# Row norms passed on by tile, first loads in order of use, multiplications by zeros there, gating's share added by itself, maxima and exponentials of the attentions in another order

## Time and profile before

| | us |
|---|---|
| median of 3 runs | 1327.89 (1327.08 to 1332.82) |
| the profiled execution, own time | 1327.28 |
| its span, first to last instruction | 1325.5 |
| TensorE busy | 1283.7 |
| VectorE busy | 933.4 |
| ScalarE busy | 692.4 |
| GpSimd busy | 30.8 |

### The profile page before, as it was taken

One profiled execution on the slowest core, in us unless ns is written; L12 is line 12 of the kernel. 1 busy time (PEld: TensorE's weight loads), 2 busy tenths in 40 slices (PEclk: granted clock), 3 DMA queues, 4 the chain that ended last, 5 costly groups with the idle time before them and its releaser, 6 DMA issues.

```text
span 1325.5 us, 21900 instructions
## 1 busy us (share of the span) xinstructions
PE 1283.7 (97%) x8592; PEld 1170.9 (88%) x8592; DVE 933.4 (70%) x1667; ACT 692.4 (52%) x1137; POOL 30.8 (2%) x26
## 2 busy tenths in 40 slices
PE   7999998999989988999999999999999999999997
PEld 6889988998878778999999999999988888888886
DVE  5766556665456756899999777777767766677766
ACT  5565556664445655444454455555554455544554
POOL 0000040000010000000000000000000000000000
PEclk9999998999999999999999999999999999999999
DMA  7533465556655435567767656565667776666663
GB/s 246 171 114 128 128 191 157 179 189 187 194 161 185 143 99 175 154 198 229 231 215 231 222 191 202 184 205 191 199 238 272 245 244 246 244 244 243 236 242 110
DMA packets 72662, 260.55 MB, mean 197 GB/s; under 512 B 8224, under 2 KB 8864, under 8 KB 72304
## 3 DMA queue, kind: packets, MB, share of 16 engines
q1 hardware_dynamic: 71232, 255.25, 58.9%
q0 software_dynamic: 1040, 3.38, 0.8%
q10 hardware_dynamic: 288, 0.52, 0.1%
HBM read 240.25 MB, written 18.87 MB: 195 GB/s over the span
## 4 chain that ended last, share of the span: by engine, by line
PE 89%; ACT 4%; DVE 4%; issue 1%; DMA 1%; SPq 0%; ACTq 0%; DVEq 0%
PE ps L937 26%; PE ps L457 15%; PE ps L465 14%; PE ps L466 14%; PE ps L467 14%; PE ps L920 2%; PE ps L500 1%; ACT whi L974 1%; DVE wlo L1407 1%; DMA X<-in_x_dram 1%; PE ps L481 1%; PE ps L475 1%; PE ps L873 1%; DMA raw<-in_w_in_dram 1%; PE ps L493 0%
## 5 line engine op out<-in xcount | busy, mean ns | idle before, releaser
L1407 DVE TENSOR_TENSOR wlo<-raw,whi 128x1024 fp32r<-128x1024 f32 (+2 forms) x411 | 499.2, 1216 | 327.0 <-ACT whi L974 324.7
L974 ACT ACTIVATE whi<-raw 128x1024 fp32r<-128x1024 f32 (+2 forms) x421 | 441.9, 1051 | 441.3 <-PE ps L937 168.6
L465 PE MATMUL ps<-TH,whi 128*128 128x256 f32 x1536 | 441.6, 287 | 2.5 <-DVE TL L1416 1.3
L466 PE MATMUL ps<-TL,whi 128*128 128x256 f32 x1536 | 434.7, 283 | 0.0
L467 PE MATMUL ps<-TH,wlo 128*128 128x256 f32 x1536 | 434.6, 283 | 0.0
L465 PEld LDWEIGHTS ps<-TH,whi 128*128 128x128 f32 x1536 | 294.8, 192 | 3.1 <-issue 3.1
L466 PEld LDWEIGHTS ps<-TL,whi 128*128 128x128 f32 x1536 | 295.0, 192 | 0.0
L467 PEld LDWEIGHTS ps<-TH,wlo 128*128 128x128 f32 x1536 | 294.7, 192 | 0.0
L937 PE MATMUL ps<-whi,TH 128*128 128x512 f32 x512 | 199.3, 389 | 1.3 <-issue 1.3
L937 PE MATMUL ps<-whi,TL 128*128 128x512 f32 x512 | 199.2, 389 | 0.0
L937 PE MATMUL ps<-wlo,TH 128*128 128x512 f32 x512 | 199.2, 389 | 0.0
(11 more groups left out here) (292 smaller groups left out, 1304.3 us busy)
## 6 DMA issues: line engine op xcount, KB each, us to landing
raw<-in_expert_u_dram SPq DMA_DIRECT2D x128, 512.0 KB, 3.7
raw<-in_expert_v_dram SPq DMA_DIRECT2D x128, 512.0 KB, 3.8
raw<-in_w_up_dram SPq DMA_DIRECT2D x32, 512.0 KB, 3.6
raw<-in_w_down_dram SPq DMA_DIRECT2D x32, 512.0 KB, 4.2
acts<-stage SPq DMA_DIRECT2D x32, 512.0 KB, 3.9
stage<-acts SPq DMA_DIRECT2D x30, 512.0 KB, 3.3
raw<-in_w_in_dram SPq DMA_DIRECT2D x20, 512.0 KB, 4.2
raw<-in_w_gate_dram SPq DMA_DIRECT2D x16, 512.0 KB, 3.4
```

Source lines behind the costliest of these rows:

```text
L465: e.matmul(dst, whi[:, h, sl], xh[:, k, :], start=k == 0, stop=False)
L466: e.matmul(dst, whi[:, h, sl], xl[:, k, :], start=False, stop=False)
L974: e.activation(whi[:, u % NH, 0:n], raw[:, u % NR, 0:n], ACT.Copy).then_inc(*hi(u))
L1407: e.tensor_tensor(wlo[:, u % NH, 0:n], raw[:, u % NR, 0:n], whi[:, u % NH, 0:n].bitcast(F32), ALU.subtract).then_inc(*lo(u))
```

## The change

1. **Start.** The constants are loaded in two parts, the identity (64 KB) first and the rest behind the fourth weight unit; x's parts and units 0 to 3 are issued in order of use. ppc is issued by ACT; positions, mask and gain vector by POOL, but only once chunk x5 is cut. ACT loads its table at once (`warm`). TensorE multiplies zeros: eight matmuls of 512 columns before the first transposes and three behind them, into a bank that is not read. x is transposed two chunks at a time, and a unit of IN_A is multiplied high part first (waiting for `hi` alone), the wlo part last.
2. **Norms "out" and "down".** The last three units do tile 0 first (`staggered_end`), then tile 1. X is transposed, cut and waited for by tile, in 128 x 128 pieces, sixteen where there were eight of 128 x 256; tile 0's transposes stand between tile 1's last matmuls. The next product begins with tile 0 alone: for UP and QUERY by `pair`, which streams 128 columns of each of two units at once against a tile of rows, and then turns the result round (`turn_paired`); for IN2 by `high_rows` and `low_rows`. The squares of the plain norm behind them move some steps later.
3. **Norm "x4"** likewise by tile, with single roots and reciprocals; QUERY + 1's low part goes to POOL.
4. **Gating's share by itself.** The norm factor of the gating half and its `fold` into X come at steps 43 to 46; b's chunks are turned into two banks and their product starts when the first is cut; the wait for v2.1 moves behind two units.
5. **Attentions.** `soft` of the second tile comes a step earlier (moba, mla, dil), ACT starts its exponentials earlier, mla is a step later in all. In dil the exponentials come at steps 31 and 32, gelu of u at 33, the gated product on DVE at 34, its transposes on TensorE at 35, ACT's second exponentials at 36 and 38.

TensorE, first block:

```diff
-LO_POOL = (BR_B + 1, BR_B + 2, BR_B + 3, OUT, OUT + 1, UP, UP + 1, IN2, IN2 + 1, QUERY)
+LO_POOL = (BR_B + 1, BR_B + 2, BR_B + 3, OUT, OUT + 1, UP, UP + 1, IN2, IN2 + 1, QUERY, QUERY + 1)
...
+            def turn_tile(name, t, chunks, src):
+                for c in chunks:
+                    b, at = tile_bank(name, t, c)
+                    if t == 0 and c >= 4:
+                        e.wait_ge(*low.at(f"{name}{c - 4}0"))
+                    elif t and c < 4:
+                        e.wait_ge(*low.at(f"{name}{c + 4}0"))
+                    e.transpose(ps[b][:, at:at + 128], src[:, t, c * 128:c * 128 + 128], ident).then_inc(
+                        *turned(f"{name}{c}{t}"))
...
+            e.wait_ge(*norm_d.at("zeros"))
+            def idle(n):
+                for _ in range(n):
+                    e.matmul(ps[7][:, :], zeros[:, 0:128], zeros[:, :], start=True, stop=True)
+            idle(8)
...
+            for c in range(2):
+                turn_x(c)
+            idle(3)
...
+            def staggered_end(name, to, u0, nu, xh, xl):
+                outs = [[ps[1][:, :]], [ps[3][:, :]]]
+                end = u0 + 2 * nu
+                for u in range(end - 3, end):
+                    whole(u)
+                    m = rows(u, 2, 512, xh, xl, outs, 2 * (u - u0 - nu), 2 * nu, [(0, 0), (1, 0)])
+                m.then_inc(*half_used(name))
+                for u in range(end - 3, end - 1):
+                    rows(u, 2, 512, xh, xl, outs, 2 * (u - u0 - nu), 2 * nu, [(0, 1), (1, 1)]).then_inc(*used(u))
+                e.wait_ge(*post_d.at(f"{name}00"))
+                turn_tile(to, 0, range(4), X)
+                rows(end - 1, 2, 512, xh, xl, outs, 2 * nu - 2, 2 * nu, [(0, 1), (1, 1)]).then_inc(*used(end - 1))
+                e.wait_ge(*post_d.at(f"{name}01"))
+                turn_tile(to, 0, range(4, 8), X)
...
+            def pair(u, name, dst, t):
+                a, b = sorted((u % NH, (u + 1) % NH))
+                sl = slice(t * 128, t * 128 + 128)
+                o = dst.rearrange("p (i n) -> p i n", i=2)
+                e.wait_ge(*hi.at(u + 1))
+                for k in range(8):
+                    w = whi[:, a:b + 1:b - a, k * 128:k * 128 + 128]
+                    e.wait_ge(*low.at(f"{name}{k}{t}"))
+                    e.matmul(o, TH[:, k, sl], w, start=k == 0, stop=False)
+                    e.matmul(o, TL[:, k, sl], w, start=False, stop=False)
+                whole(u)
+                whole(u + 1)
+                for k in range(7):
+                    e.matmul(o, TH[:, k, sl], wlo[:, a:b + 1:b - a, k * 128:k * 128 + 128], start=False, stop=False)
...
+            pair(UP, "h2.", ps[0][:, 0:256], 0)
+            e.wait_ge(*post_d.at("out10"))
+            turn_tile("h2.", 1, range(4), X)
+            e.wait_ge(*post_d.at("out11"))
+            turn_tile("h2.", 1, (4, 6, 5, 7), X)
+            pair(UP, "h2.", ps[1][:, 0:256], 1)
```

TensorE, steps of the second block:

```diff
                     for hp in range(4):
                         e.wait_ge(*soft_d.at(f"dil0{head_at(hp, 1)}"))
                         score_pair(dil, 1, hp).then_inc(*scored(f"dil1{hp}"))
+                elif s == 35:
                     e.wait_ge(*gelu_a.at("ug1"))
                     e.wait_ge(*ln_d.at("gated1"))
```

TensorE, norm x4:

```diff
+            rows(OUT2 + 7, 2, 512, TH, TL, outs_b[1], 2, 4, [(0, 1)])
+            e.wait_ge(*norm_d.at("x4.00"))
+            turn_tile("x4.", 0, range(4), xn3)
+            rows(OUT2 + 7, 2, 512, TH, TL, outs_b[1], 2, 4, [(1, 1)]).then_inc(*used(OUT2 + 7))
+            e.wait_ge(*norm_d.at("x4.01"))
+            turn_tile("x4.", 0, range(4, 8), xn3)
```

ScalarE, `row_norm` and steps of the second block:

```diff
+                e.wait_ge(*half_used.at(name))
+                root(0)
+                split(end)
+                high_tile(to, 0, range(4), gain)
+                split(end + 1)
+                high_tile(to, 0, range(4, 8), gain)
+                e.wait_ge(*used.at(end - 1))
+                root(1)
+                split(end + 2)
+                high_tile(to, 1, range(8), gain)
...
+                elif s == 31:
+                    exps(dil, 0, range(4))
+                elif s == 32:
+                    exps(dil, 0, range(4, 8))
                 elif s == 33:
-                    exps(dil, 0, range(4))
-                elif s == 34:
-                    exps(dil, 0, range(4, 8))
+                    gelu("ug", ug, 2, sums_u, IN2 + 15)
+                elif s == 36:
+                    exps(dil, 1, range(4))
                     e.wait_ge(*turned.at("A"))
```

ScalarE, norm x4:

```diff
             last_half(0, 0)
+            last_half(0, 1)
+            last_root(0)
             last_half(1, 0)
+            split(QUERY)
+            high_tile("x4.", 0, range(4), gain_x4)
+            split(QUERY + 1)
+            high_tile("x4.", 0, range(4, 8), gain_x4)
```

VectorE, steps of the second block:

```diff
-                elif s == 32:
+                elif s == 33:
+                    soft(dil, 1)
+                elif s == 34:
                     e.wait_ge(*gelu_a.at("ug1"))
                     e.wait_ge(*ln_d.at("mixed1"))
                     for t in range(2):
                         m = e.tensor_tensor(tmp3[:, t, :], tmp3[:, t, :], ug[:, t, :], ALU.mult)
                     m.then_inc(*ln_d("gated1"))
-                elif s == 34:
-                    soft(dil, 1)
```

SyncE, first loads:

```diff
-            e.dma_start(cst[:, :], A["cst"]).then_inc(*d_cst(0))
+            e.dma_start(ident, A["cst"][:, 0:128]).then_inc(*d_ident(0))
             load_x(0, 0, 256)
-            e.dma_start(posi[:, :], A["positions"]).then_inc(*d_pos(0))
             load(0)
+            load(1)
             load_x(1, 256, 512)
+            load(2)
             load_x(2, 512, 1024)
-            for u in range(1, QUERY + 4):
+            load(3)
+            e.dma_start(cst[:, 128:CST_W], A["cst"][:, 128:CST_W]).then_inc(*d_cst(0))
+            for u in range(4, QUERY + 4):
                 load(u)
```

More of the change, by code:

```diff
@@ new lines, in tensor_program @@
+            whole(OUT2 + 4)
+            for j in range(2):
+                e.wait_ge(*low.at(f"B{j}"))
+                m = rows(OUT2 + 4, 2, 512, TH, TL, outs_b[0], 0, 4, both(j))
+            m.then_inc(*used(OUT2 + 4))
+            e.wait_ge(*low.at("B3"))
+            for i in range(1, 4):
+                whole(OUT2 + 4 + i)
+                m = rows(OUT2 + 4 + i, 2, 512, TH, TL, outs_b[i // 2], i % 2 * 2, 4, [(0, 0), (1, 0)])
+                if i % 2:
+                    m.then_inc(*half_used(f"out2{i // 2}"))
@@ L1711, in row_norm @@
                 update(0, 0)
+                update(0, 1)
+                split(end)
+                low_tile(to, 0, range(4), gain)
+                split(end + 1)
+                low_tile(to, 0, range(4, 8), gain)
                 gained(1, 1)
@@ L1887, in vector_program @@
+            split(QUERY + 2)
+            low_tile("x4.", 1, range(8), gain_x4)
             e.tensor_copy(keys[:, :], cs("iota")).then_inc(*route_d("keys"))
@@ L2119, in pool_program @@
             split(QUERY)
[L2120 removed]
+            split(QUERY + 1)
+            e.wait_ge(*low.at("x4.71"))
             e.dma_start(sub[:, :, :], A["sub_keys_2"]).then_inc(*d_sub(0))
```

667 lines of the change are left out of this document (381 added, 286 removed), and 12 rows, old and new, of tables (high, low, turned).

## The result

| | before | after |
|---|---|---|
| median of 4 runs, us | 1327.92 (1327.08 to 1332.82) | 1314.39 (1314.17 to 1314.88) |
| span of the profiled execution | 1325.5 | 1312.5 |
| mean granted clock | 0.993 | 0.997 |

The ratio is 0.9891 (95% interval 0.9867 to 0.9915): 1.1% faster, 13.5 us. The forecast was 1314. The total is right, by luck: of its parts mla has the wrong sign (3.1 off), and start, dil and x4 miss by 1.5 to 2.7, on both sides.

What follows compares the result with a forecast made beforehand. TensorE was taken as the bound, busy 1283.7 of 1325.5 us. Terms 5.1 + 2.7 + 4.4 + 3.9 + 1.0 - 4.0 = 13.1 off 1327.28 gave 1314 us; range 1304 to 1321.

Steps and rivals of the forecast that it cites:

- Start: Kernel start: first unit lands earlier and the loop over IN_A ends at 22.5 instead of 27.74, 5.1 us gained.
- landing term: Start: less data ahead of IN_A's first unit, so it lands at 5.2 and TensorE starts near 6.5 us.
- moba: moba attention: soft a step earlier removes waits of 1.0 and 0.7 us; net gain 1.5 us.
- mla: mla attention: moving its steps by one removes two waits of 0.6 us, 1.2 us gained.
- "out": Norm "out": 7.3 us lost now, 2.5 stay, turning adds 0.5, clock stays full; 4.4 us gained.
- "down" with its squares: Norm "down": 6.3 us lost becomes 2.4, 3.9 gained; moved squares remove the wlo wait, 1.0 gained.
- dil: Dilated attention: new order makes TensorE wait 5.9 us for the gated product, clock falls (2.5); 4.0 us lost net.
- b and x4: Gating's b product and norm x4: b gains 0.9 us, x4 loses 0.4 and 0.5 for the clock; nothing in sum.
- 1 (no stall in dil): Rival: dil's stall isn't there and "x4" gains too, giving 1307 us; chance 0.2.
- 2: Rival: small pieces cost each norm 1.8 us more and the clock falls again, giving 1319 us; chance 0.2.
- 3: Rival: TensorE waits for tile 1 as before, so "out" and "down" give nothing, 1322 us; chance 0.08.
- 4: Rival: `pair`'s two-buffer operand streams slowly, giving 1326 us, or 1344 at four times 0.12; chance 0.02.

Runs made afterwards that it cites:

- mla2: Changed kernel with mla's last three exponentials (ACT) one step earlier and its last transposes of probabilities (TensorE) one step later: 1311.85 us.
- no_stagger: Changed kernel without the staggered ends of OUT and DOWN, so no rows of tile 1 are held back: 1322.15 us.
- fill_turns: Changed kernel with 28 useless transposes of 128 columns in TensorE's wait for dil's gated product: 1312.36 us.
- x4_order: Changed kernel with ACT and DVE cutting tile 0's chunks before tile 1's square and mean at norm x4: 1313.03 us.

## Why the prediction was right in sum, and where not

- **Start, forecast 5.1, measured 3.3.** The loop over IN_A ended near 23.3 (its last matmul starts at 23.12) instead of 27.74; I had 22.5. The step that failed is "5.1 gained" as the gain of the whole stage: of the loop's 4.4, 0.86 is lost again at the next unit. Another 0.3 went in the same stretch (the matmul for `rbc`, which moved from inside the loop to step 13, is in it); it was not separated. The landing term was sound (first product 7.20, and 6.5 to 7.0 in other profiles with the same loads and zeros, for my 6.5). Taking the new loads away costs 3.0 of the stage, taking the zeros away 1.3.
- **moba 1.5, measured 1.9:** right in size.
- **mla, forecast 1.2 gained, measured 1.9 lost: the wrong sign.** The step that failed is "mla's step removes two waits of 0.6", with nothing put against it. TensorE's and DVE's steps moved by one while ACT's last exponentials kept their place, and I never laid ACT's list beside them: they stand behind a tanh that waits for TensorE. A new wait of 2.0 ate the gain (0.35 lost where the clock stays), and in half of the profiles the clock fell too, 1.5 more in the one compared here. mla2 shows that 0.9 over the kernel before was to be had.
- **"out" 4.4, measured 3.8; "down" with its squares 4.9, measured 5.7.** Right, and the clock stays as said. A 128 x 128 cut in a row is 0.28 on either engine, for my 0.31. X's first half came 2.3 after tile 0's sums (194.02 to 196.29), as I had it; but the row that I took it from says 2.8 (200.48 and 1.25 make 201.73), as it holds the collision with POOL, which I passed over. no_stagger shows that the gain hangs on the held rows, as the working had it, and also that it hangs on POOL's timing, which the working lacked.
- **dil -4.0, measured -1.3.** The mechanism is right, three of its sizes are off. The stall is 4.3 for 5.9: 1.28 of table load had been counted in series, and TensorE came 0.5 later than I had it. The clock took 1.6 for 2.5 (fill_turns). The removed waits gave 4.6 for 4.4: 2.17 by v2.1, and, as what is left of the stage, 2.4 by the maxima and tmp.
- **b and x4: 0, measured 1.5.** b's wait fell from 1.9 to 0.96 as said. x4's mechanism is right (TensorE waits for tile 0's chunks behind the other tile's square), but the wait is 1.9 and 0.45 where I had 3, and POOL's and tile 1's part was 0.89 and 0.94 where I had 0.6 and 2.4. The clock stayed in the compared profile; where it fell there, in four of eleven, it cost under 0.1 us, for my 1.
- **The rivals.** 1 (no stall in dil) fell by the 4.3. 2 fell by the windows at the norms, all at 1.00, and by the 0.28 of a piece; its price was also too low, since 5.4 is its 1.8 at three norms and leaves out its own 4 for the clock (1323, outside the range). 3 is what no_stagger nearly makes of the kernel, not the change. 4: `pair`'s matmuls start 0.12 apart.

So 1314 came out by luck, through errors that cancel: start 1.8 and mla 3.1 too good, dil 2.7 and x4 1.5 too bad. Two terms are also 0.1 off their own working (start 27.74 - 22.5 = 5.2, "out" 7.3 - 2.5 - 0.5 = 4.3), and these cancel too.

## What to carry to other kernels

When steps of one engine are shifted by one, lay the other engines' lists beside it and ask of each instruction what it now stands behind; a wait for TensorE inside ACT's list makes everything behind it late. Passing a norm on by tile paid here only with work held back to cover it: without the held rows under 1 us of 9.5 was left, in part because POOL's work then collided with DVE's. Where the clock falls in some runs and not in others, compare the length of the stage in the trace, not the medians: 1.5 us came and went here with the same instructions. And look at what the stage waits for before a half clock is priced: at x4 it was free.

## What was not expected of the hardware

- A DVE update with two SBUF operands that starts while POOL's subtraction runs waits for it: 2.84 and 2.85 for 0.75 us at the two norms of no_stagger, 1.25 at "out" in the kernel before, and it ended 0.55 or 0.56 after POOL each time. DVE's cuts out of PSUM, with one SBUF operand, took 0.28 each beside the same POOL instruction in the changed kernel. "SBUF — State Buffer" of the Trainium skill ("Who interferes with whom") has the rule, a lock on a shared port for DVE instructions with two SBUF inputs against GpSimd's reads; this trace agrees.
- The clock can fall behind a wait of 2.0 us, or behind waits of 0.39 and 0.71 with a run of 64-column matmuls, and the same program with the same waits may keep it: five of ten profiles at mla, four of eleven at x4 behind 1.7. A fall took 1.2 to 1.6 us at mla and dil where the half clock lasted 3.41 (mla 54.10 to 54.39 for 52.88), 2.5 to 2.7 where it lasted 6.83 (dil 30.9 and 31.0 for 28.45 in mla2 and x4_order, mla 55.56 in x4_order), and under 0.1 at x4.
- An activation's table load runs ahead of what the activation itself waits for: at dil it was over at 435.66, 3.15 us before the maxima were there (438.81).
